# Prompt attention of a hybrid decoder layer: float32r scores on 64 rows, one query tile per round, scaling on GpSimd

## The reference

```python
D_MODEL, SEQ, HEAD_DIM = 1024, 2048, 64      # 8 dilated heads, 4 differential heads
# dilated: softmax(q k + log of how many of three dilated windows read the key) v, per head
# differential, two maps per head, values of 128:
sc = jnp.einsum('nqhce,nkhce->nhcqk', q, k).astype(jnp.float32) * (e ** -0.5)
a = jax.nn.softmax(jnp.where(valid, sc, -jnp.inf), axis=-1)
wts = a[:, :, 0] - lam * a[:, :, 1]
return jnp.einsum('nqhk,nkhe->nqhe', wts, v.astype(jnp.float32))
```

## Time and profile before

| | |
|---|---|
| median of 3 runs | 4602.29 us (4599.25 to 4607.43) |
| profiled execution, its span | 4601.9 us |
| project | 0 to 713 us |
| attend_prompt, dilated | 713 to 1300 us (17 us of it first loads) |
| attend_prompt, differential | 1300 to 1797 us |
| attend_decode and mlp | 1797 to 4602 us |
| TensorE busy, whole span | 90% |

### The profile page before, as it was taken

One profiled execution on the slowest core, in us unless ns is written; L12 is line 12 of the kernel. 1 busy time (PEld: TensorE's weight loads), 2 busy tenths in 40 slices (PEclk: granted clock), 3 DMA queues, 4 the chain that ended last, 5 costly groups with the idle time before them and its releaser, 6 DMA issues. The chain is left out here.

```text
span 4601.9 us, 72420 instructions
## 1 busy us (share of the span) xinstructions
PE 4152.4 (90%) x22272; PEld 3160.3 (69%) x22272; DVE 2403.4 (52%) x5184; ACT 1536.3 (33%) x2569; POOL 805.8 (18%) x694
## 2 busy tenths in 40 slices
PE   7996998999989897888888879999999998999998
PEld 6875884445444444445444458988988997998898
DVE  3333334756677684444444435565565555555654
ACT  2221224555545443223322332233223223223322
POOL 0001000000000000333333322222222222222121
PEclk9997999999999998999999989999999999999999
DMA  5756623110111103999999953324333333332231
GB/s 187 234 194 211 228 76 86 36 37 8 36 35 37 36 10 114 376 330 350 365 348 349 360 171 120 116 95 128 127 100 113 124 110 103 125 118 99 94 125 61
DMA packets 347208, 686.79 MB, mean 149 GB/s; under 512 B 27769, under 2 KB 185465, under 8 KB 343610
## 3 DMA queue, kind: packets, MB, share of 16 engines
q1 hardware_dynamic: 291295, 448.03, 29.3%
q0 software_dynamic: 47488, 218.01, 13.3%
q10 hardware_dynamic: 8155, 17.77, 1.4%
HBM read 632.85 MB, written 117.70 MB: 163 GB/s over the span
## 5 line engine op out<-in xcount | busy, mean ns | idle before, releaser
L1379 POOL TENSOR_TENSOR d_up_lo<-d_up_raw,d_up_hi 128x2048 fp32r<-128x2048 f32 x100 | 460.6, 4606 | 1420.3 <-ACT d_up_hi L1516 1420.3
L1384 PE MATMUL d_ups<-d_a_hi,d_up_hi 128*128 128x416 f32 x1600 | 568.2, 355 | 16.9 <-DVE d_a_lo L1671 16.2
L1386 PE MATMUL d_ups<-d_a_hi,d_up_lo 128*128 128x416 f32 x1600 | 566.1, 354 | 0.0
L836 POOL DMA_DIRECT2D c_v<-in_v_cache x512 | 275.2, 537 | 1638.9 <-issue 1627.8
L1385 PE MATMUL d_ups<-d_a_lo,d_up_hi 128*128 128x416 f32 x1600 | 560.6, 350 | 0.0
L530 PE MATMUL b_s<-b_k,b_q 128*128 128x512 f32 (+3 forms) x1280 | 498.5, 547 | 54.1 <-DVE b_part L662 30.6
L1384 PE MATMUL d_dps<-d_u_hi,d_down_hi 128*128 128x416 f32 x1280 | 461.7, 361 | 57.6 <-DVE d_y L1696 55.8
L1696 DVE TENSOR_TENSOR d_y<-d_y,d_dps 128x416 f32<-128x416 f32 x640 | 367.9, 584 | 225.6 <-PE d_dps L1386 223.6
L1386 PE MATMUL d_dps<-d_u_hi,d_down_lo 128*128 128x416 f32 x1280 | 458.2, 358 | 0.0
L1385 PE MATMUL d_dps<-d_u_lo,d_down_hi 128*128 128x416 f32 x1280 | 454.0, 355 | 0.0
L530 PEld LDWEIGHTS b_s<-b_k,b_q 128*128 128x128 f32 x1280 | 236.6, 197 | 291.0 <-issue 191.1
(11 more groups left out here) (164 smaller groups left out, 6306.4 us busy)
## 6 DMA issues: line engine op xcount, KB each, us to landing
c_k<-in_k_cache SPq DMA_DIRECT2D x512, 256.0 KB, 6.2
c_v<-in_v_cache POOLq DMA_DIRECT2D x512, 256.0 KB, 5.7
d_down_raw<-in_w_down SPq DMA_DIRECT2D x80, 1024.0 KB, 5.1
d_up_raw<-in_w_up SPq DMA_DIRECT2D x80, 1024.0 KB, 7.3
out_ka_win<-in_ka_state POOLq DMA_DIRECT2D x8, 4064.0 KB, 14.6
out_va_win<-in_va_state POOLq DMA_DIRECT2D x8, 4064.0 KB, 26.5
d_up_raw<-in_w_out SPq DMA_DIRECT2D x20, 1024.0 KB, 7.5
a_x<-in_x_prompt SPq DMA_DIRECT2D x32, 512.0 KB, 4.1
```

The source lines that it names most:

```text
L836: eng.dma_start(dst[i][:, g, :], io[src[0]][bass.ds(page, 1)].rearrange("o p d -> (o p) d")).then_inc(landed[i], 16)
L1379: nc.gpsimd.tensor_tensor(up_lo[i][:], up_raw[i][:], up_hi[i][:].bitcast(F32), ALU.subtract).then_inc(up_lo_ready, 1)
L1384: nc.tensor.matmul(dst, w_hi, x_hi, start=first, stop=False)
L1386: return nc.tensor.matmul(dst, w_lo, x_hi, start=False, stop=last)
```

## The change

In `project` the turned q and k are kept as two float32r parts: ScalarE's copy rounds to the high part, and VectorE subtracts it from the turned PSUM tile for the low part, at the end of each step. Both are stored, so `qT` and `kT` are twice as large. TensorE's next turns and SyncE's stores wait for the subtraction.

`attend_prompt` is written anew, without loops: 128 rounds, 8 pairs by 16 query tiles. A round handles one query tile and both heads (or both maps) of a pair.

- Scores: q and k of the two heads lie on rows 0 to 63 and 64 to 127; each block of up to 512 keys takes three float32r products per head, issued in turn for the two heads, each into its own PSUM bank.
- TensorE's order in round m interleaves, block by block, the scores of tile m+2, the transposes of tile m, and the products of tile m. A transposed bank holds four key tiles of one query tile; the product moves 128 queries at a time.
- VectorE takes scores two rounds ahead, forms one shift for both maps, inverts both sums in one instruction (`invert`), and, for differential heads, subtracts the second map (`combine`).
- ScalarE in round m: copies of bank 0 of tile m, exp of map 0 of tile m+1, copies of bank 1, exp of map 1, then the other copies.
- GpSimd scales the weights by the inverted sums: both rows of a dilated tile, the first map's row of a differential tile.
- The causal table shrinks from 2048 to 1024 columns. SyncE loads q by tile (four deep), k and v by chunks of 512 keys (six deep). VectorE starts after both tables have landed.

```diff
-        zT = [sb(f"a_zT{b}", [P, NR, NP, P]) for b in range(2)]
+        zT = [sb(f"a_zT{b}", [P, NR, NP, 2, P], F32R) for b in range(2)]
...
+                    for i in range(NR):
+                        dve.wait_ge(zT_ready, n * NR + (2 + i + 1))
...
+                        nc.vector.tensor_tensor(zT[b][:, i, :, 1, :], z_turn[i % 2][:, :].rearrange("p (g n) -> p g n", g=NP),
+                                                zT[b][:, i, :, 0, :].bitcast(F32), ALU.subtract).then_inc(zT_split, 1)
...
+    AHEAD, WR = 2, 3
+    SS, TS, WS = 2, 3, 4
+    KR, QR = 6, 4
...
+                    for i, (ql, kl) in enumerate(((0, 0), (0, 1), (1, 0))):
+                        for mm in range(2):
+                            h = slice(mm * HD, (mm + 1) * HD)
+                            ins = nc.tensor.matmul(s_ps[mm][e % SS][:, 0:cols], q[n % QR][h, ql, :],
+                                                   k[chunk(n, b) % KR][h, kl, 0:cols], start=(i == 0), stop=(i == 2))
...
+                for m in range(-AHEAD, STEPS):
+                    fore = m + AHEAD
+                    for b in range(NT // CB):
+                        if fore < STEPS and b < blocks(fore):
+                            score(fore, b)
+                        if m >= 0 and b < blocks(m):
+                            turns(m, b)
+                            if b:
+                                product(m, b - 1)
+                    if m >= 0:
+                        product(m, blocks(m) - 1)
...
+                for m in range(-AHEAD + 1, STEPS):
+                    for b in range(NT // CB):
+                        if m >= 0 and b < blocks(m):
+                            copies(m, b)
+                        if b < 2 and m + 1 < STEPS:
+                            weights(m + 1, b)
...
+                for n in range(STEPS):
+                    pool.wait_ge(inverted, n + 1)
+                    for mm in range(1 if diff(n) else 2):
+                        row = w[n % WR][mm][:, 0:(tile_of(n) + 1) * P]
+                        ins = nc.gpsimd.tensor_scalar(row, row, inv[:, n % WR, mm:mm + 1], None, ALU.mult)
...
+                def invert(n):
+                    dve.wait_ge(exp_done, 2 * n + 2)
...
+                def combine(n):
+                    if not diff(n):
+                        return
...
+                    dve.wait_ge(scaled, diffs(n + 1))
...
+                for m in range(-AHEAD, STEPS):
+                    fore = m + AHEAD
+                    half = min(2, blocks(fore)) if fore < STEPS else 0
+                    for b in range(half):
+                        take_scores(fore, b)
+                    if 0 <= m + 1 < STEPS:
+                        invert(m + 1)
+                    if fore < STEPS:
+                        for b in range(half, blocks(fore)):
+                            take_scores(fore, b)
+                        find_shift(fore)
+                    if 0 <= m + 1 < STEPS:
+                        combine(m + 1)
```

More of the change, by code:

```diff
@@ L316, in prologue @@
                 def prologue():
+                    dve.sem_inc(zT_split, 2)
                     dve.wait_ge(const_in, 64)
@@ L454, in attend_prompt @@
         o_out = [sem(f"b_o_out{i}") for i in range(2)]
[L455 to L463, removed]
-                self.n = len(self.units)
-                self.part0 = [sum(NQ * (g + 1) * len(self.maps) for _, _, g in self.units[:n]) for n in range(self.n + 1)]
-                self.key0 = [sum(NQ * (g + 1) for _, _, g in self.units[:n]) for n in range(self.n + 1)]
-                self.rows = NQ * len(self.maps)
-                self.links = sum(self.rows * (g > 0) + (3 if diff else 1) * NQ for _, _, g in self.units)
-            def halved(self, g):
-                return not self.diff and g > 0
@@ L475, in attend_prompt @@
[L475 to L489 removed]
+        vec, vec_gate = sem("b_vec"), sem("b_vec_gate")
@@ new lines, in attend_prompt @@
+        pair_of = lambda n: n // NT
+        tile_of = lambda n: n % NT
+        diff = lambda n: pair_of(n) >= NP
+        blocks = lambda n: tile_of(n) // CB + 1
+        block0 = [sum(map(blocks, range(n))) for n in range(STEPS + 1)]
+        banks = lambda n: blocks(n) * (1 if diff(n) else 2)
+        bank0 = [sum(map(banks, range(n))) for n in range(STEPS + 1)]
+        diffs = lambda n: max(0, n - NP * NT)
+        chunk = lambda n, b: pair_of(n) * (NT // CB) + b
+        wide = lambda n, b: min(512, (tile_of(n) + 1) * P - b * 512)
@@ new lines, in _ @@
+                for n in range(QR, STEPS):
+                    load_q(n)
+                    ahead = n - QR
+                    if ahead % NT == 1 and 0 < pair_of(ahead):
+                        for c in range(CB * pair_of(ahead) + 2, min(CB * pair_of(ahead) + 6, CB * NPAIR)):
+                            load_k(c)
+                    if ahead % NT == 3 and 0 < pair_of(ahead):
+                        for c in range(CB * pair_of(ahead) + 2, min(CB * pair_of(ahead) + 6, CB * NPAIR)):
+                            load_v(c)
@@ L636, in _ @@
                 link = linker(dve, vec, Count(0))
-                for m in range(2):
-                    nc.vector.memset(q[0][(1 - m) * HD:(2 - m) * HD, m, :], 0.0).then_inc(zeroed, 1)
                 dve.wait_ge(lam_in, 16)
@@ new lines, in combine @@
+                def combine(n):
+                    if not diff(n):
+                        return
+                    cols = (tile_of(n) + 1) * P
+                    dve.wait_ge(inverted, n + 1)
+                    dve.wait_ge(scaled, diffs(n + 1))
+                    row = w[n % WR][0][:, 0:cols]
+                    nc.vector.scalar_tensor_tensor(out=row, in0=w[n % WR][1][:, 0:cols], scalar=inv[:, n % WR, 1:2],
+                                                   in1=row, op0=ALU.mult, op1=ALU.add).then_inc(w_ready, 1)
```

432 lines of the change are left out of this document (193 added, 239 removed).

## The result

The changed kernel takes 4963.52 us (median; 4961.47 to 4965.84) against 4602.81 us before: a ratio of 1.0782, with a 95% interval of [1.0767, 1.0797], 361 us slower.

What follows compares the result with a forecast made beforehand. TensorE bounds `attend_prompt` (1067 us); after the change a serial chain of 984 us plus 30 for the clock makes 1014, a gain of 53. 4601.9 - 53 + 6 + 2 = 4557 us, range 4470 to 4820.

Steps and rivals of the forecast that it cites:

- The bound and its replacement: In `attend_prompt`: TensorE bounds now (878 of 1067 us); after, at 692 us, it yields to a serial chain of 984.
- Scores side by side: In `attend_prompt`: two heads' score products run together on their 64 rows, 196 us instead of 392.
- rival 3: Two heads' score products run one after the other: TensorE 888 us, kernel 4587 us, chance 0.06.
- The chain without the scaling: Serial waits over the 128 rounds of `attend_prompt`, without GpSimd's scaling and the clock: 735 us.
- copies ahead of the second exp: ScalarE's copies that precede the second exp in each round of `attend_prompt`: 144 us in the chain.
- first transposes, inverting and all hand-overs: Chain terms per round: first bank's transposes on TensorE 79 us, inverting and hand-overs between engines 89 us.
- First round and last copies: Chain time outside the rounds: first round, last copies and products, and VectorE being late: 27 us.
- GpSimd's scaling: GpSimd scaling 192 rows of weights: 249 us, half the two-input cost, between 183 (memset) and 498 (two-input operation).
- The clock: TensorE slowing to 1.2 GHz after idle gaps, making first bank's transposes longer: 30 us, bounds 0 to 77.
- Rival 2: GpSimd scales near its two-input pace, 350 to 498 us: kernel 4658 to 4853 us with half-clock stretches, chance 0.29.
- First loads and `project`: VectorE's wait for both tables adds 6 us (0 to 12); the two subtractions in `project` add 2.
- Stages behind "start as before": Stages following `attend_prompt` were said to start as before; no time was added for them.

Runs made afterwards that it cites:

- the clock held up: Changed kernel, TensorE repeating the first block's high-by-high score products for about 60% of each wait for GpSimd: 4886.50 us.
- the run on it: Changed kernel with only the shift's 128x2 multiplication moved from VectorE to ScalarE: 4980.09 us, 1.0811 of the kernel before.
- the better order: Changed kernel with both exps ahead of the copies and inverting behind the first score block: 4578.18 us; with the shift on ScalarE as well, 4544.64 us.

## Why the prediction was wrong, step by step

- **The bound and its replacement: right.** In the stage TensorE's busy share fell to 69%, its waits end on GpSimd and on `combine`, and two thirds of its score products are worth 25 us. TensorE's own work was somewhat under-sized: a full dilated block (scores, eight transposes, sixteen products, with their changes of shape) takes 0.90 + 1.02 + 1.02 = 2.94 us in the timeline at full clock, where the sum had 0.82 + 1.00 + 0.95 = 2.77. So it was for the kernel before: by the earlier trace rows TensorE idled for 92 of the 1067 us there, and the sum left 189.
- **Scores side by side: right**, and rival 3 with it wrong. Six products of 512 columns and the change of shape take 0.90 us; in turn the products alone would take 6 x 0.24 = 1.44.
- **The chain without the scaling, 735 us: right in its rows.** Exps 308 (309 summed), `combine` 86.5, as before. As a whole: with the clock held up the stage is 1337 us, and 735 + 579 = 1314; 23 us are left for all that the sum missed. The timelines of that run, followed from one tile's finished weights to the next tile's, show the terms one by one: copies ahead of the second exp 145 us (144 summed), exps 309 (309), and first transposes, inverting and all hand-overs 205 (79 + 89 = 168). First round and last copies are 12 (27). So the chain was read rightly, and its 23 us are mostly 37 too little in transposes and hand-overs and 15 too much outside the rounds.
- **GpSimd's scaling, 249 us, bounds 183 to 498: this is the step that failed.** It measured 579, 330 more than was taken and 81 beyond the upper bound. The bound came from an assumption that no row supports: that an operation with one input can't cost more than one with two on the same engine. It does, 5441 ns against 4606. What tipped the choice was the same thought ("its second read falls away"). The Trainium skill, "GPSIMD Engine Reference", § Engine selection, has one-input work roughly at line rate; the copy, 1891 ns for 2048 columns, agrees with that, and the multiplication, 2.9 times as long, does not. The Trainium skill, "GPSIMD Engine Reference", § Key points, has VectorE about twice as fast, which pointed the right way, and the trace has 4.2.
- **The clock, 30 us, bounds 0 to 77: under-sized.** 75 us came back with the clock held up. It was sized on waits of 2 us per round; with GpSimd's true price they are up to 7.9 us. It was also looked for in the wrong place: the prediction slowed the first bank's transposes, and from finished weights to the first copy the clock cost 24 us (158 against 134 with the clock held up), but from there to the end of the second exp, where ScalarE waits for the later banks, 54 (199 against 145, exps left out).
- **Rival 2 was what happened**, beyond its own end: it gave 2.7 us for a 2048 row as the point from which the kernel is slower, and 5.4 is twice that. Even its half-clock end, 4853, lies under what was measured, because its GpSimd too stopped at 498 us. By its formula, 735 + 579 + 75 = 1389 in place of 1067, and 8 for the other edits: 4601.9 + 322 + 8 = 4932. The span is 4959.9; the 28 left are the 23 of the chain, 7 in the stages behind, and -2 that `project` didn't cost.
- **First loads and `project`: right.** +5.5 against +6; `project` ends 0.2 us earlier than before (+2). **Stages behind "start as before"**: decode and `mlp` take 7 us more. In the profiles of all kernels here they take between 2801 and 2812 us, with no pattern in what GpSimd or the order did, so the 7 us lie within that spread, and what makes it stays open.
- **What the argument left out:** GpSimd's rows hold small VectorE instructions. In the changed kernel that costs next to nothing, as the run on it shows; in the better order it cost some 34 us.

## What to carry to other kernels

An operation that no row shows on an engine has no upper bound from another operation on that engine, however much more that one reads: with 1.9 us (copy), 4.6 (two inputs, stored as float32r) and 5.4 (one input and a scalar) for the same 2048 columns the number of streams did not tell the price here. Work that is moved to an idle engine is free only if it leaves the path: here nearly all of the 579 us were links of a chain of waits. The chain was about as much to blame as the price: two changes of order alone (exps ahead of the copies, inverting behind the first block) took 385 us off with GpSimd still scaling, and the scaling on VectorE with the first of them gave 4473 us.

## What the runs showed of the hardware that was not expected

- GpSimd's multiplication of float32 by a constant or by a scalar per partition goes at 2.54 ns a column (5365 to 5442 ns for 2048), slower than its subtraction of two tiles stored as float32r (4606) and 2.9 times its copy (1891).
- A VectorE instruction can be held while GpSimd's instruction runs, however small it is: 5.25 us for a copy of 128x2. Held were a copy and a multiplication by a constant on two columns, and beside an instruction of GpSimd that reads, a product of two tiles; not held were reductions, reciprocals and two multiplications of one column. The Trainium skill, "SBUF — State Buffer", § SBUF: two separate sides, has a port pair that VectorE and GpSimd share as an exclusive lock for the whole instruction, taken on VectorE's side by its faster modes, and by instructions with two inputs from SBUF only against a GpSimd operation that reads SBUF. The runs agree on the last point: 3.51 us beside the multiplication, 0.16 beside the memset. They differ on the length for that product: it was let go 1.71 us before GpSimd's row ended, which is not explained.
- After a wait of 5.18 us TensorE's next 3.5 us had a granted clock of 0.50, the level of 1.2 GHz; products of no use in about 60% of the waits kept the stage at 0.98 and 0.97 and made it 75 us shorter, though TensorE did more.
